# The order of two inner loops in the Strassen products of a two-branch mixer kernel

## The reference

```python
def mixer_layer(x, conv_buf, s_prev, pos, g, w_in, conv_w, w_a, w_r, w_o, log_gamma):
    h = rmsnorm(x, g)
    p = h @ w_in                       # 1024 x 9216, the largest product
    hc, b, c, z_a, q, k, v, z_r, g_a, g_r = jnp.split(p, split_at, axis=-1)
    u = c * hc                         # causal conv of width 3, gated
    a = ((b * conv(u)) * silu(z_a)) @ w_a
    o, s_new = retention(rotary(q), rotary(k), v, s_prev, log_gamma)
    r = (head_norm(o) * silu(z_r)) @ w_r
    merged = sigmoid(g_a) * a + sigmoid(g_r) * r
    return x + merged @ w_o, new_buf, s_new
```

## Time and profile before

| what | value |
|---|---|
| median of 3 runs | 2303.63 us (2303.25 to 2304.83) |
| profiled execution, first to last instruction (span) | 2304.0 us |
| mean granted TensorE clock of the profiled execution | 0.996 |
| TensorE matmuls busy | 2281.5 us (99%), 17005 instructions |
| TensorE weight loads busy | 2260.4 us (98%), 17005 instructions |
| DVE busy | 1377.8 us (60%) |
| ACT busy | 870.1 us (38%) |
| POOL busy | 903.7 us (39%) |

### The profile page before, as it was taken

The page is one execution under the profiler, slowest core; times in us unless marked ns, Lnnn a source line. Parts: engine busy times, 40 slices in busy tenths (PEclk is TensorE's granted clock), DMA queues, the critical chain, the costliest instruction groups (busy, mean ns, idle before and its releaser), DMA issues.

```text
span 2304.0 us, 40644 instructions
## 1 busy us (share of the span) xinstructions
PE 2281.5 (99%) x17005; PEld 2260.4 (98%) x17005; DVE 1377.8 (60%) x1486; ACT 870.1 (38%) x1366; POOL 903.7 (39%) x603
## 2 busy tenths in 40 slices
PE   7999999999999999999999999999999999999998
PEld 7999999999999999999999999999999999999998
DVE  6776777556663565743476776774566526556334
ACT  6433333344444444322233333334334444333133
POOL 3555665565555300000047556554665551000000
PEclk9999999999999999999999999999999999999999
DMA  9322122233333565554452222223343326656444
GB/s 298 86 66 67 55 75 65 71 129 133 124 105 114 200 211 194 182 170 124 133 172 75 66 61 61 66 65 114 125 133 112 99 94 237 219 195 200 124 151 133
DMA packets 260519, 294.06 MB, mean 128 GB/s; under 512 B 9032, under 2 KB 218224, under 8 KB 260336
## 3 DMA queue, kind: packets, MB, share of 16 engines
q1 hardware_dynamic: 260176, 291.40, 39.0%
q10 hardware_dynamic: 160, 0.05, 0.0%
HBM read 206.84 MB, written 84.57 MB: 126 GB/s over the span
## 4 chain that ended last, share of the span: by engine, by line
PE 94%; issue 2%; POOL 1%; DVE 1%; DMA 1%; ACT 0%; SPq 0%; DVEq 0%; POOLq 0%; ACTq 0%
PE ps L1608 61%; PE ps L1650 21%; PE ps L1869 3%; PE ps L1597 2%; PE ps L1659 1%; PE ps L1657 1%; PE ps L1658 1%; PE ps L1754 1%; PE ps L1699 1%; PE ps L1688 1%; DMA w_raw<-in_w_in_dram 1%; POOL s_lo L691 0%; DVE t_lo L1145 0%; PE ps L1670 0%; PE ps L1738 0%
## 5 line engine op out<-in xcount | busy, mean ns | idle before, releaser
L1608 PE MATMUL ps<-t_hi,s_lo 128*128 128x272 f32 x3808 | 788.2, 288 | 0.0
L1608 PE MATMUL ps<-t_hi,s_hi 128*128 128x272 f32 x3808 | 787.4, 288 | 0.5 <-ACT snap L838 0.5
L1608 PE MATMUL ps<-t_lo,s_hi 128*128 128x272 f32 x3808 | 785.1, 288 | 0.0
L1608 PEld LDWEIGHTS ps<-t_hi,s_hi 128*128 128x128 f32 x3808 | 598.8, 188 | 0.9 <-issue 0.9
L1608 PEld LDWEIGHTS ps<-t_lo,s_hi 128*128 128x128 f32 x3808 | 598.4, 189 | 0.0
L1608 PEld LDWEIGHTS ps<-t_hi,s_lo 128*128 128x128 f32 x3808 | 594.4, 189 | 0.0
L1178 DVE TENSOR_TENSOR e<-ps,snap 128x544 f32<-128x544 f32 x272 | 195.9, 723 | 518.7 <-PE ps L1608 390.1
L691 POOL TENSOR_TENSOR s_lo<-w_pair,s_hi 128x512 fp32r<-128x512 f32 x136 | 229.8, 1690 | 321.5 <-ACT s_hi L828 321.5
L838 ACT ACTIVATE snap<-ps 128x544 f32<-128x544 f32 x272 | 169.2, 622 | 433.1 <-PE ps L1608 432.7
L828 ACT ACTIVATE s_hi<-w_pair 128x512 fp32r<-128x512 f32 x204 | 127.7, 629 | 169.3 <-PE ps L1608 167.2
L702 POOL TENSOR_TENSOR sA<-w_pair 128x512 f32<-128x512 f32 x68 | 89.4, 1314 | 220.3 <-DVE s_lo L1166 220.3
(11 more groups left out here) (242 smaller groups left out, 3724.4 us busy)
## 6 DMA issues: line engine op xcount, KB each, us to landing
w_pair<-in_w_in_dram SPq DMA_DIRECT2D x136, 512.0 KB, 5.0
w_raw<-in_w_o_dram SPq DMA_DIRECT2D x24, 512.0 KB, 5.2
xs<-x_keep SPq DMA_DIRECT2D x16, 544.0 KB, 5.4
prod_keep<-e SPq DMA_DIRECT2D x16, 544.0 KB, 2.7
v_keep<-e SPq DMA_DIRECT2D x16, 544.0 KB, 6.7
z_keep<-e SPq DMA_DIRECT2D x16, 544.0 KB, 3.8
prod_raw<-prod_keep SPq DMA_DIRECT2D x16, 544.0 KB, 6.4
vT<-v_keep SPq DMA_DIRECT2D x16, 544.0 KB, 7.4
```

The source lines that it names most:

```text
L1608: i = mm(ps[:, r + p, 0:PART], s[j][:, k, :], b[operand][:, k, p * PART:(p + 1) * PART], start=(FRESH[j] and k == 0 and t == 0), stop=(k = ...
```

## The change: which of two loops is the inner one

In `product` the loop over the two column parts p becomes the outer one of the two loops inside k, and the loop over the three terms t the inner one.

```diff
                 for k in range(4):
-                    for t, (s, b) in enumerate(((s_hi, t_hi), (s_hi, t_lo), (s_lo, t_hi))):
-                        for p in range(2):
+                    for p in range(2):
+                        for t, (s, b) in enumerate(((s_hi, t_hi), (s_hi, t_lo), (s_lo, t_hi))):
                             i = mm(ps[:, r + p, 0:PART], s[j][:, k, :], b[operand][:, k, p * PART:(p + 1) * PART],
                                    start=(FRESH[j] and k == 0 and t == 0), stop=(k == 3 and t == 2),
                                    skip_group_check=True)
```

## The result

The changed kernel takes 2312.92 us (median of 5 runs, 2311.49 to 2313.22), the kernel before 2303.80 us (5 runs, 2303.25 to 2304.83): ratio 1.0037, 95% interval 1.0027 to 1.0048. It is slower by 9.1 us. "No change", 2303.6 us, was forecast; the rival by the parts had been priced at +10.3 us.

A forecast was written before the change was run, and what follows sets the result against it. It took L1608's dense matmul stream, 61% of the span at 125.32 ns pitch, as the bound. Its terms summed 0 + 0 + 0 + 0, leaving 2304.0 us profiled and a 2303.6 us median; the range reached 2315 and a gain below 4 us.

The forecast's parts named there:

- the rival by the parts: L1608, between successive matmuls: alternating column parts saves 1.35 ns, four of six steps lose it; +10.3 us, 2313.9 us; chance 0.20.
- (a): TensorE's waits at the head of each product: t_lo and s_lo are used earlier but already awaited; cost 0.
- (b): L1608: three matmuls in a row add into the same bank instead of alternating; cost 0, bound 9.1 us either way.
- (c): L1608's weight loads: stationary tile changes in 4 of 6 matmuls instead of 2; cost 0, bound 0.8 us either way.
- (d): L1608: alternating column parts might explain 1.35 ns saved per matmul; taken as 0, ends +15.4 and -11 us.

The follow-up runs named there:

- e2: Changed kernel with results sent to the two banks in turn again, operand order kept: 711.50 us for 5640 matmuls, 2313.26 us in one run.
- e3: Kernel before with only the weights in the changed kernel's order (hi, hi, lo, hi, hi, lo): 706.81 us for 5640 matmuls, 2304.86 us in all.
- e15: Changed kernel reading only pieces 0 and 1 of t_hi, in turn throughout: 3041 ns per product, 2317.72 us in all.
- e1: Kernel before with the two column parts, and their banks, taken as 1, 0 instead of 0, 1: 3054 ns per product, 2325.49 us in all.
- e13: Changed kernel reading piece 1 of t_hi in all 24 matmuls of a product: 3041 ns per product, 2318.80 us in all.
- e17: Changed kernel reading piece 1 of t_hi in all 24 matmuls, every stationary tile shifted by 64 bytes: 3041 ns per product, 2317.69 us.
- e18: Changed kernel reading piece 0 of t_hi in all 24 matmuls, every stationary tile shifted by 192 bytes: 3041 ns per product, 2319.78 us.
- e5: Changed kernel, banks and weights kept, moving pieces read by address (t_hi, t_lo, t_hi): 705.24 us for 5640 matmuls, 2301.26 us in all.
- e6: Changed kernel with t_hi read in place of t_lo: 711.50 us for 5640 matmuls, 2312.36 us in all.
- e7: Kernel before with t_hi read in place of t_lo: 706.81 us for 5640 matmuls, 2303.60 us in all.
- e9: Changed kernel reading piece 5 i mod 8 of t_hi for the i-th matmul: 705.24 us for 5640 matmuls, 2299.74 us in one run.
- e12: Changed kernel reading piece 0 of t_hi in all 24 matmuls: 707.12 us for 5640 matmuls, 2304.13 us in one run.
- e16: Kernel before with the term loop outside the k loop, timed in 12 runs: median 2303.72 us, ratio 1.000; layers 705.24 and 709.93 us.
- e4: Kernel before with the term loop outside the k loop, column parts innermost: 705.24 us for 5640 matmuls, 2300.70 us in all.
- e8: Kernel before with the term loop outside k and L1650's units cut 352 + 352 + 384 columns: 2295.54 us in 6 runs, ratio 0.9970.
- e11: Changed kernel reading piece 2 i mod 8 of t_hi for the i-th matmul: 705.24 us for 5640 matmuls, 2300.62 us in one run.

## Why the prediction was wrong

**(a) The waits: right.** Idle time before L1608 is 1.0 us, under the bound of 5 us.

**(b) The banks: right.** e2 undoes the new order of the banks and leaves 711.50 us. The zero that had been read from the 384-column and the 320-column rows holds for this order at 272 columns.

**(c) The weights: right.** e3 makes the new order of weights alone and gives 706.81 us, the kernel before to the hundredth. The advice that the prediction took from the Trainium skill ("TensorE: Matmul & The Clock Gate", step-by-step list of what each phase is for), to load once and multiply repeatedly, has nothing to act on where every matmul has its own load; e3 shows no price for a change.

**(d) The alternation of the parts: the step that failed.** It was rated 0, with +15.4 and -11 us as ends, "because the gate units, with other tiles in another order and four banks, come out at 125.5 ns, 0.2 ns away". The term measured +9.5 us. The gate units were no test of it: they read pieces 0, 1 in turn just as the old product does, so they shared with it the very thing that the change was to remove. The rows at 384 and 320 columns, held against the rival, were no test either: their pieces begin at 0, 1536 and 3072 bytes, all multiples of 256, so there the place modulo 256 never changes. Of three things moved, the nearest rows had covered two; for the third only rows with the same pattern as before were at hand, and their agreement was taken as freedom from the pattern. The prediction had seen that 1.35 ns per matmul were unexplained, that this happened at this width only, and that the amount went with k; a remainder that one can't explain, in the group that the change rearranges, deserved more than 0.20.

**The rival by the parts: right in place, near in size, wrong in mechanism.** Its place (between successive matmuls of L1608), its price (+10.3 us against +9.5) and its sign (a pitch of 126.2 or over; 126.15 measured, just at the bound) came out. That alternation is what saves did not: alternation alone is slow (e15, 714.61 us), alternation in the other phase slower still (e1, 717.70 us). The near hit is luck. The "saving" against the line of the other widths is real as a number, since e13, e15, e17 and e18 stand right on that line (3041 / 24 = 126.7 ns), but it is not alternation's: piece 0 alone, without any alternation, is at 125.4 ns.

**The range** ended at 2315.0 and held the result; the forecast of no change, at 0.62, failed.

**What is shown and what is open.** Shown: the loss comes with the sequence in which the moving operand's pieces are read (e5 takes it back with banks and weights as changed; e2 and e3 leave banks and weights no part), the 8704 bytes between the tiles have no part (e6, e7), nor has going on at the next address (e9); the place of the stationary operand counts as well (e18); and the price of a sequence is not the sum of prices of its steps (e12 to e15). That what counts of the sequence is where the pieces begin modulo 256 bytes fits all of these runs and is what they leave, each on one execution. Open: the rule by which a sequence comes out at its number. One regularity stands in the rows: 2988, 3008, 3021, 3028, 3041 and 3054 ns lie within 0.4 ns of 3001 plus -2, 1, 3, 4, 6 and 8 times 6.67 ns, which is 16 columns at 2.4 GHz, the step that fits the widths at L1650 too; only piece 0 alone (3009.0) is off it. That the same code ran at two of these numbers in one execution (e16) would fit two periodic reads that can lock together in more than one way, but no run tests that.

## What to carry to other kernels

Where TensorE is dense and every wait is gone, its matmuls still carry a remainder, 11 to 14 ns over the streaming time in the pairs of these runs, and which moving pieces come in which order, with widths and counts unchanged, moves it by up to 2.8 ns per matmul (702.12 to 717.70 us for 5640), 2% of the stage. Cut widths into whole multiples of 16 fp32 columns, and let pieces begin at multiples of 64 bytes, first: that gave 1.3% of its stage in a profiled execution, and with the other order 0.3% of the kernel in six timed runs. Then try orders on the chip, look at both layers and at many runs, and don't trust a gain that only one of them has. When a row is used as evidence that an order is free, check that it does not share with the old order the thing that is to change.

## What was unexpected about the hardware

Rearranging 24 matmuls with the same operands, banks, loads and waits changes their time by -0.2% to +1.5% (3001 to 3054 ns against 3008); with pieces chosen freely it goes down to 2988. The numbers come back to 0.01 us in 705: e4, e5, e8, e9, e11 and the first layer of e16 all have 705.24. Piece 0 repeated is 1.1% quicker than piece 1 repeated, and a shift of the weights by 192 bytes undoes that. In one kernel the same code ran at two paces in the two layers of one execution, and its runs spread over 11.5 us where those of the kernel before spread over 2.7.
